# Two hybrid layers and a mixture of experts on one core: narrower waits of the scores, softmax steps of two units moved, two column loads issued by SyncE

## The reference

```python
for l in range(2):
    proj = rmsnorm(x, norm_g[l]) @ w_in[l]                   # 256 x 5824
    ya = sliding-window attention: 8 query heads, 2 key heads, ALiBi slopes, a sink per head
    yb = latent attention: 4 heads; q and kv are projected up again from ranks 384 and 256, 64 rope columns
    yc = differential attention: 4 heads, two softmaxes per head, exp1 - lambda * exp2, then rmsnorm
    y  = concatenate([ya * silu(a_g), yb * silu(b_g), yc * silu(c_g)])
    x  = x + y @ w_out[l]                                    # 256 x 2048
x = rmsnorm(x, final_norm)
# second block: mod = silu(c) @ ada_w + ada_b (2048 -> 12288), split into shift, scale, gate (twice);
# h = rmsnorm(x) * (1 + scale1) + shift1; gated delta network + two attentions; 32 experts, 2 per token
```

## Time and profile before

| | us |
|---|---|
| median of three executions | 2583.55 |
| the profiled execution, its own time | 2587.33 |
| its span, first to last instruction | 2585.4 |
| TensorE busy | 2420.2 (94%) |
| VectorE, ScalarE, GpSimd busy | 837.4, 798.7, 910.6 |
| layer 0 and layer 1, on the profile's clock | about 25 to 534, and 534 to 1003 |

### The profile page before, as it was taken

How to read it: one execution, slowest core, us unless ns; L and a number is a source line. 1 busy time by engine, 2 the same in 40 slices (tenths; PEclk the granted TensorE clock), 3 DMA queues, 4 the chain that set the end, 5 groups by cost and what they waited for, 6 DMA issues and landing times.

```text
span 2585.4 us, 30068 instructions
## 1 busy us (share of the span) xinstructions
PE 2420.2 (94%) x12151; PEld 1557.2 (60%) x12151; DVE 837.4 (32%) x1353; ACT 798.7 (31%) x1453; POOL 910.6 (35%) x409
## 2 busy tenths in 40 slices
PE   7999999999999997999989797999999999999997
PEld 5667677875676686777777676544444444444443
DVE  4142643122244446247363643111111211111113
ACT  4334444533344443442222533211111112111111
POOL 5455655855565569674343164000000000000000
PEclk9999999999999998999999798999999999999999
DMA  8666665585666552441222236699999999999994
GB/s 324 245 267 275 240 253 224 212 327 204 260 261 248 225 228 93 163 163 66 83 83 105 92 148 278 260 417 428 429 428 429 429 428 429 428 429 429 428 429 201
DMA packets 58492, 716.41 MB, mean 277 GB/s; under 512 B 10416, under 2 KB 10832, under 8 KB 14752
## 3 DMA queue, kind: packets, MB, share of 16 engines
q1 hardware_dynamic: 51664, 710.48, 67.5%
q10 hardware_dynamic: 6032, 2.88, 0.4%
q0 software_dynamic: 704, 1.75, 0.2%
HBM read 710.85 MB, written 4.24 MB: 277 GB/s over the span
## 4 chain that ended last, share of the span: by engine, by line
PE 50%; issue 38%; DVE 7%; POOL 2%; ACT 2%; ACTq 0%; DMA 0%; DVEq 0%; POOLq 0%
PE bank L1869 16%; PE bank L344 8%; PE bank L1880 8%; PE bank L354 4%; PE bank L1918 3%; PE bank L1837 2%; POOL weight_ring_parts L1794 1%; PE bank L1970 1%; PE bank L1953 1%; PE bank L1936 1%; PE bank L434 1%; PE bank L440 1%; PE bank L553 1%; DVE x_res L1081 1%; ACT w_hi_parts L2097 1%
## 5 line engine op out<-in xcount | busy, mean ns | idle before, releaser
L1794 POOL TENSOR_TENSOR weight_ring_parts<-weight_ring,w_hi_parts 128x1024 fp32r<-128x1024 f32 (+2 forms) x368 | 874.1, 2396 | 665.6 <-ACT w_hi_parts L2097 664.9
L2097 ACT ACTIVATE w_hi_parts<-weight_ring 128x1024 fp32r<-128x1024 f32 (+2 forms) x368 | 375.4, 1042 | 500.4 <-PE bank L1880 222.6
L1212 POOL TENSOR_TENSOR rms_out<-rms_in,minus_half 128x2 f32<-128x2 f32 x2 | 1.4, 696 | 980.0 <-DVE rms_in L1500 968.0
L1292 PE MATMUL bank<-weight_ring,qk_t 128*64 128x512 f32 x1024 | 224.2, 593 | 7.9 <-DMA weight_ring<-in_expert_w_up_dram 7.9
L1869 PE MATMUL bank<-w_hi_parts,h_t_parts 128*128 128x512 f32 (+1 forms) x768 | 217.0, 407 | 6.6 <-ACT w_hi_parts L2097 6.6
L1869 PE MATMUL bank<-w_hi_parts,x_res_parts 128*128 128x512 f32 (+1 forms) x768 | 201.6, 387 | 0.0
L1880 PE MATMUL bank<-weight_ring_parts,h_t_parts 128*128 128x512 f32 (+1 forms) x768 | 193.6, 381 | 0.0
L1292 PEld LDWEIGHTS bank<-weight_ring,qk_t 128*64 128x64 f32 x1024 | 76.7, 137 | 152.2 <-issue 152.2
L1869 PEld LDWEIGHTS bank<-w_hi_parts,h_t_parts 128*128 128x128 f32 x768 | 134.6, 193 | 54.5 <-issue 20.1
L1869 PEld LDWEIGHTS bank<-w_hi_parts,x_res_parts 128*128 128x128 f32 x768 | 143.3, 192 | 30.5
L1880 PEld LDWEIGHTS bank<-weight_ring_parts,h_t_parts 128*128 128x128 f32 x768 | 140.3, 189 | 28.9
(11 more groups left out here) (450 smaller groups left out, 3550.2 us busy)
## 6 DMA issues: line engine op xcount, KB each, us to landing
weight_ring<-in_w_in_dram SPq DMA_DIRECT2D x64, 2048.0 KB, 7.9
weight_ring<-in_ada_w_dram SPq DMA_DIRECT2D x48, 2048.0 KB, 11.7
weight_ring<-in_expert_w_gate_dram SPq DMA_DIRECT2D x32, 2048.0 KB, 26.9
weight_ring<-in_expert_w_up_dram SPq DMA_DIRECT2D x32, 2048.0 KB, 16.9
weight_ring<-in_expert_w_down_dram SPq DMA_DIRECT2D x32, 2048.0 KB, 22.7
weight_ring<-in_w_out_dram SPq DMA_DIRECT2D x24, 2048.0 KB, 7.9
proj<-in_expert_w_gate_dram SPq DMA_DIRECT2D x16, 2048.0 KB, 25.4
proj<-in_expert_w_down_dram SPq DMA_DIRECT2D x16, 2048.0 KB, 19.8
```

The source lines that it names most:

```text
L1292: last = mm(bank[side][s, :], m.xg[:, 8 * j + k, s], weights(hu + e, 8)[:, k, :], start=j == 0 and k == 0, stop=j == 1 and k == 7)
L1794: nc.gpsimd.tensor_tensor(weights(split, True), weights(split, False), rounded(split).bitcast(f32), ALU.subtract)\
L2097: A_(rounded(split), weights(split, False), ACT.Copy).then_inc(w_hi_ready, 1)
```

## The change

It has four parts.

1. `scores` no longer calls `copied()`. Each turning of queries and keys goes through `qk_columns`, which notes for its group ("M", "D", "W", and "W1" for window heads 4 to 7) the count of `ta_copied` and `td_copied` that its last turning on either bank will give. `scores` waits for these two counts. The `ada` product is no longer among them.
2. `FIXED` of unit 11: both steps of `soft` W2 stand ahead of pieces 2 and 3 in place of 3 and 4. `FIXED` of unit 12: the four steps of `out` W2 stand ahead of pieces 3, 4, 4, 5 in place of 2, 3, 3, 4, and `y` 0 and 1 ahead of 5 and 6 in place of 4 and 5.
3. The output pairs turned in unit 11 come in the order 5, 4, 7, 6 in place of 4, 5, 6, 7; the places are 6, 7, 7, 8 as before.
4. The two column loads of layer 1 are issued by SyncE, right behind the second `ada_w` half of unit 6, and no more by ScalarE behind unit 2.

```diff
--- before.py
+++ after.py
@@ -85,11 +85,11 @@
 UNIT_TASKS = {4: [("mla_rope", 0)], 5: [("soft", "M0"), ("soft", "M1")], 6: [("out", "M0"), ("prep_d", 0)],
               7: [("gates_d", 0), ("out", "M1"), ("soft", "D0"), ("soft", "D1")], 8: [("out", "D0"), ("soft", "D2"), ("out", "D1")],
               9: [("soft", "D3"), ("out", "D2"), ("prep_w", 0)], 10: [("out", "D3"), ("soft", "W0"), ("soft", "W1"), ("out", "W0")],
-              11: [("prep_w", 1), ("soft", "W2"), ("out", "W1"), ("y", (4, 5, 6, 7))],
+              11: [("prep_w", 1), ("soft", "W2"), ("out", "W1"), ("y", (5, 4, 7, 6))],
               12: [("soft", "W3"), ("out", "W2"), ("y", (0, 1)), ("out", "W3"), ("y", (2,))], 13: [("y", (3,))]}
 FIXED = {4: (1, 2, 3, 4, 5, 6), 5: (2, 3, 4, 5), 6: (1, 2, 2, 3, 4, 5, 6, 7), 7: (1, 2, 2, 3, 4, 5, 6, 7), 8: (2, 3, 4, 5, 6, 7),
-         9: (2, 3, 4, 5, 5, 6, 7), 10: (1, 2, 2, 3, 4, 5, 6, 7, 7, 8), 11: (1, 2, 3, 4, 4, 5, 5, 6, 6, 7, 7, 8),
-         12: (1, 2, 2, 3, 3, 4, 4, 5, 6, 7, 7, 8, 8), 13: (2,)}
+         9: (2, 3, 4, 5, 5, 6, 7), 10: (1, 2, 2, 3, 4, 5, 6, 7, 7, 8), 11: (1, 2, 2, 3, 4, 5, 5, 6, 6, 7, 7, 8),
+         12: (1, 2, 3, 4, 4, 5, 5, 6, 6, 7, 7, 8, 8), 13: (2,)}
 X_AT = {0: (14, 1), 1: (14, 5), 2: (15, 4), 3: (0, 4)}
 
 
@@ -1754,6 +1754,11 @@
                         sp.wait_ge(pc_used, l * NPC)
                     sp.dma_start(uq, a["mla_w_uq"][l].rearrange("(k p) n -> p k n", p=P)).then_inc(mla_in, 16)
                     sp.dma_start(ukv, a["mla_w_ukv"][l].rearrange("(k p) n -> p k n", p=P)).then_inc(mla_in, 16)
+                if l == LAYERS - 1 and s == 6 and j == 1:
+
+                    sp.wait_ge(mod_out, 16 * 12)
+                    for dst, at in ((m.shc, 0), (m.gsc, D)):
+                        sp.dma_start(dst[:, :], mod[0, at:at + D].rearrange("(k p) -> p k", p=P), allow_slow_non_contiguous=True).then_inc(m.cols_in, 16)
             else:
                 h = key[2]
                 half(key, w_out_d[l, OUT_HALVES[h][0], OUT_HALVES[h][1]])
@@ -1828,6 +1833,7 @@
         s, o, e, c = Tally(0, 1), Tally(0, 1), Tally(), Tally()
         e_of = {}
         x_done, y_done = {}, {}
+        qk_turned = {}
 
         def transposes(by_act, sources):
 
@@ -1920,10 +1926,17 @@
                 last.then_inc(ada_used, 1)
             td.next()
 
+        def qk_columns(by_act, group, sources):
+
+            transposes(by_act, sources)
+            qk_turned[group, by_act] = (ta if by_act else td).now()
+
         def scores(kind, h, comp):
             pe.wait_ge(s_used, s.now())
             s.next()
-            copied()
+            group = "W1" if kind == "W" and h >= 4 else kind
+            pe.wait_ge(ta_copied, qk_turned[group, True])
+            pe.wait_ge(td_copied, qk_turned[group, False])
             for t in range(TT):
                 out = psS[:, t * S:(t + 1) * S]
                 tok = slice(t * P, (t + 1) * P)
@@ -1997,7 +2010,7 @@
 
         def rope_queries(l):
             pe.wait_ge(rope_ready, l + 1)
-            transposes(True, [ropeq[:, t, 2 * i:2 * i + 2, :] for i in (0, 1) for t in range(TT)])
+            qk_columns(True, "M", [ropeq[:, t, 2 * i:2 * i + 2, :] for i in (0, 1) for t in range(TT)])
 
         def evacuated(l, v, do):
             pe.wait_ge(pj_copied, 16 * l + v)
@@ -2011,13 +2024,14 @@
                 if kind == "mla_rope":
                     for x, width in ((mlaq, 192), (mlakv, S)):
                         for h in (0, 2):
-                            do.append(lambda h=h, x=x, width=width: evacuated(l, 8, lambda: transposes(
-                                h == 0, [x[:, t, (h + i) * width:(h + i) * width + P] for i in (0, 1) for t in range(TT)])))
-                    do += [lambda: rope_queries(l), lambda: transposes(False, [kr2[:, t, :, :] for t in range(TT)])]
+                            do.append(lambda h=h, x=x, width=width: evacuated(l, 8, lambda: qk_columns(
+                                h == 0, "M", [x[:, t, (h + i) * width:(h + i) * width + P] for i in (0, 1) for t in range(TT)])))
+                    do += [lambda: rope_queries(l), lambda: qk_columns(False, "M", [kr2[:, t, :, :] for t in range(TT)])]
                 elif kind in ("prep_d", "prep_w"):
                     cols = (DQ, DQ + 2 * P, DK, DK + 2 * P) if kind == "prep_d" else ((AQ, AQ + 2 * P, AK), (AQ + 4 * P, AQ + 6 * P))[arg]
-                    do = [lambda i=i, at=at: evacuated(l, v, lambda: transposes(
-                        i % 2 == 0, [PROJ[:, t, at + b * P:at + (b + 1) * P] for b in (0, 1) for t in range(TT)]))
+                    group = "D" if kind == "prep_d" else ("W", "W1")[arg]
+                    do = [lambda i=i, at=at, group=group: evacuated(l, v, lambda: qk_columns(
+                        i % 2 == 0, group, [PROJ[:, t, at + b * P:at + (b + 1) * P] for b in (0, 1) for t in range(TT)]))
                           for i, at in enumerate(cols)]
                 elif kind == "gates_d":
                     do = []
@@ -2262,10 +2276,6 @@
                     task(l, kind, arg)
                 split_to(q + sum_place(p) + AHEAD)
                 store_row(l, p)
-                if l == LAYERS - 1 and p == 2:
-                    act.wait_ge(mod_out, 16 * 12)
-                    for dst, at in ((m.shc, 0), (m.gsc, D)):
-                        act.dma_start(dst[:, :], mod[0, at:at + D].rearrange("(k p) -> p k", p=P), allow_slow_non_contiguous=True).then_inc(m.cols_in, 16)
             out = l < LAYERS - 1
             split_to(q + FIRST[13] + 1 + AHEAD)
             for kind, arg in UNIT_TASKS[13]:
```

## The result

The changed kernel takes 2554.52 us (median of 4 runs, 2551.98 to 2557.03). The kernel before, on the same chip, takes 2584.72 (4 runs, 2583.14 to 2589.29). The ratio (an estimate from the runs, not the quotient of the two medians) is 0.9878, with a 95% interval of 0.9865 to 0.989: faster by 1.2%. The medians lie 30.2 us apart, where 31.5 us and 2552 us were forecast. The profiled execution took 2551.98 us with a span of 2550.1, against 2587.3 and 2585.4 of before: 35.3 us between these two.

The account below looks back on a forecast made before the run. TensorE, busy 94% of the span, bounds the kernel, so only its waits and low clock count. 12.8 + 9.35 + 3.0 + 6.3 = 31.5 us off the median 2583.55 gives 2552 us, range 2546 to 2563.

Parts of the forecast that it names:

- 5.91, 4.71 and 2.2 us: Gains from narrower score waits: unit 9 in layer 1, unit 9 in layer 0, unit 12 in both layers; sum 12.8 us.
- rival a: Layers: the low clock falls as often behind other, shorter waits; 9.3 us stay, 2561 us; chance 0.12.
- 1.60 + 1.63: Slow clock given back behind old product waits, in us: unit 11 of layer 0, unit 12 of layer 1.
- 3.0 and 1.4: Unit 11, layers 0 and 1: us gained by moved steps, 1.4 per layer plus layer 0's slow clock of 1.60.
- the new wait: Unit 11: first scores of W2 would wait 1.07 us for VectorE's copy of their queries.
- 1.66 and 3.29: Behind unit 11, layers 0 and 1: us gained at W2's product, 1.66 per layer plus layer 1's slow clock of 1.63.
- I take 0: Unit 10's row store, some 4 us later, was costed at nothing; other end 3 us per layer.
- some 16 us for an issue of 7: SyncE between units 6 and 7, layer 1: a gap of some 16 us for column loads needing 7 us to issue.
- rival (b): SyncE's queue: column elements delay the half of unit 7; 7 us back, 2559 us; chance 0.10.
- (c): Units 11 and 12: moved steps give nothing, through ScalarE's roundings or the late row store; 9.35 us lost, 2561; chance 0.08.
- (d): The gain is lost in a later stage that does not begin with TensorE; 2583 us; chance 0.05.
- (e): SyncE's queue: elements far slower, unit 7's half late by d; slower by 0.3% from 44 us, 2657 possible; chance 0.03.

Follow-up runs that it names:

- part 1 alone: The kernel before with only the scores waiting for no more than their own columns' copies: 2574.03 us, ratio 0.9966.
- part 2 alone: The kernel before with only the steps of units 11 and 12 moved a piece earlier or later: 2576.34 us, ratio 0.997.
- part 4 alone: The kernel before with only the two column loads of layer 1 issued by SyncE in place of ScalarE: 2578.01 us, ratio 0.9974.
- columns in a quiet moment: The kernel before with the column loads still on ScalarE but issued 23 us earlier, ahead of the MLA up projection: 2578.02 us, ratio 0.997.
- the early store: The changed kernel with the row store of unit 10 issued ahead of the output pairs of unit 11: 2550.50 us, ratio to before 0.986.
- part 3 alone: The kernel before with only the output pairs of unit 11 turned in the order 5, 4, 7, 6: 2595.41 us, ratio 1.004, slower.

## Why the prediction was right, step by step

**Part 1: right.** Of 5.91, 4.71 and 2.2 us, 5.92, 4.73 and, in part 1 alone, twice 1.1 were measured against the same trace of before. The stretch had been read as a whole from one scores to the next, so that the slow matmuls were in the sum from the start. The mechanism is shown. The agreement to the hundredth is luck in part: five profiled executions have the old code in unit 9, and in layer 1 they took 36.84, 35.64, 35.67, 36.92 and 35.64 us, so 1.2 us of the 5.91 belong to the execution that was read.

**The clock (rival a): given back, but only on the whole.** All five slow stretches of the forecast are gone in the profiled execution of after, whose granted clock is 1.00 there. But they are chance in part: part 2 alone left unit 9 of layer 0 at 35.64 us and part 4 alone at 37.25, and unit 9 of layer 1, 36.84 us in before, took 35.67 and 35.64 in them, with the same code throughout. Each such stretch is 1.2 to 1.6 us. The second block's 1565.3 to 1573.3 us is the larger noise, and the sums of medians of the parts alone are good to some 5 us only.

What is not chance shows when two places are taken together. Three executions have the old code in units 11 and 12 (before, part 4 alone, columns in a quiet moment). In layer 0 unit 11 took 39.05, 37.47 and 37.48 us, and the stretch behind it 129.02, 130.60 and 130.64; the sums are 168.07, 168.07 and 168.12. In layer 1 the sums are 155.82, 155.79 and 155.89. Each time one slow stretch of 1.6 us stood behind one of the two waits for `p_t`, now the first and now the second. So the forecast's 1.60 + 1.63, one per layer, was sound although each of the two places was chance.

**Part 2: right.** Unit 11 gave 3.06 and 1.46 us against 3.0 and 1.4; within it the new wait was 0.87 and not 1.07 us, and the leftover of 0.2 us was let in as 0.3. In unit 12, too, the product's leftover was 0.2 us, with 0.35 let in. Behind unit 11 part 2 alone gave 1.83 and 3.42 us against 1.66 and 3.29, so it is not part 2 that leaves the table short by 0.80 and 0.92 us there in the full change; it is the next point.

**Part 3: the gain right, its side cost wrong.** The `ada` product's 1.5 us per layer came back. The step that failed is "I take 0" for the late row store. The text had the delay right (three roundings and a copy), and the measured 1.4 us per layer lies inside its other end of 3. What it did not follow to its end was the second instruction of that step: the store is followed by the load of the next bias on the same queue, and it is that load for which VectorE waits. It was issued at 868.20 and used at 874.85, 6.65 us for 2 KB, while the weights' halves were in flight (421 GB/s from 873 on). A price was to hand, 9.5 us for the column loads under such traffic, and from 868.20 it would have put the row some 6 us behind the end of the `ada` product (867.83 + 3.64 = 871.47). Measured: VectorE starts the row 5.59 - 2.38 = 3.2 us late, TensorE waits 1.4 us per layer, of which the early store gives back 1.05. It did no more harm only because of part 1. Without it the same lateness costs 4.52 - 1.11 = 3.4 us of wait in layer 0 and slow matmuls, and the kernel is slower than before (part 3 alone). The forecast's sum treats the parts as independent; it came out right for the full change, and would not have for part 3 alone, where it said 3.0 us faster and 10.8 slower was measured. The working of part 3 does not say that its price rests on part 1; as far as that was not seen, the sum is luck.

**Part 4: the result right, the margin wrong.** 6.48 us for 6.3. But "some 16 us for an issue of 7" took ScalarE's 6.90 us for a price of the load, when it was what remained of the halves' traffic (5.8 us) and a little more. Issued right behind the halves, with 11.8 us of them to go, it took 14.28. It ended at 677.70 + 14.28 = 691.98, and the next half was issued at 693.00. So the gap had 1.0 us to spare, not 9, and rival (b) was near. The half was not late: it was issued 13.98 us before TensorE took it at 706.98, where the earlier trace rows had 13.97. A late one would still have had the margin at the other end: ScalarE began to round that half at 700.63, some 5 us ahead of what TensorE needed. Moving the loads later (1.03 us) or to a quiet moment on ScalarE (3.76) gives the same time with more room.

That last series bears on the page of the Trainium skill that the forecast weighed, "DMA: Bandwidth & Descriptors", section "Issuing engines are not separate DMA queues", by which spreading issues over engines saves only issue time, usually small beside the transfer. Here the issue of one load was 1.03 of 4.0 us until landing with the halves landed, and 3.76 of 6.4, 6.90 of 9.5 and 14.28 of 16.7 us with weight halves in flight: the last three are not small. That only issue time is saved agrees: what part 4 gained is the wait behind ScalarE's 6.90 us with the slow matmuls after it, and ScalarE at a better moment gave the same 2578.0 us as SyncE, so the gain needed another moment or another engine, not the engine as such.

**Rivals (c), (d), (e).** (c) is part of what happened, at about 2 us in place of 9.35. For (d): the second block kept the whole 33.5 us. For (e): the elements landed after 16.7 us, and the half of unit 7 was late by nothing, where d would have had to be 36 us.

## What to carry to other kernels

Where a wait is by one running count for many consumers, look for a consumer that needs less: here scores stood 3.1 us for a row they never read, and the slow matmuls behind the wait cost 1.6 to 2.8 us more. When a step is moved, follow each instruction it issues to the one that needs it, and price a small transfer by what is in flight, not by its size. Edits that meet at one late item may have no price of their own: part 3 cost 10.8 us alone and none beside part 1, so try the set before dropping a part. And where the low clock counts, take two places with like waits together, and more than one execution.

## What was not expected of the hardware

- How long an engine is held by issuing a load of 2048 single elements (8 KB) went with what was left of the 2 MB halves in flight: 1.03, 3.76, 6.90, 13.89 and 14.28 us in five kernels, landing after 4.0, 6.4, 9.5, 16.3 and 16.7. In the four with halves in flight it ended 1.2 to 2.8 us behind the fall of their rate, on ScalarE as on SyncE.
- A load of 2 KB took 6.65 us from issue to use while the halves were moving.
- The same code at the same place ran with slow matmuls in one execution and without them in the next (unit 9 of layer 0: 35.64 and 37.25 us), so a single trace prices the low clock to within 1.6 us per stretch. The sum over the two like places of a layer repeated to 0.1 us.
